# Up projections by feature with high and low tokens side by side, their halves summed in the eviction

## What is computed

```python
def sq_relu_mlp(h, w1, w2):                  # both layers of the first block; D_FF = 4096
    return jnp.square(jax.nn.relu(h @ w1)) @ w2

# second block, token mixer: three convolution inputs of 512 features each
proj = h @ w_in[l]
b_gate, c_gate, hc, q, k, v = jnp.split(proj, splits, axis=-1)
u = c_gate * hc                              # then a causal convolution of 3 taps
y = b_gate * conv(u)

# second block, PEER: product keys
q = (ht @ wq).reshape(t, PEER_HEADS, 2, PEER_DK)      # 2048 features
sa = jnp.einsum('thd,hnd->thn', q[:, :, 0], keys[0])
sb = jnp.einsum('thd,hnd->thn', q[:, :, 1], keys[1])
# top 16 of each, top 16 of their sums; then gelu(u_tab[i] . h) weights rows of v_tab
```

## Time and profile before

| | |
|---|---|
| time, median of 3 | 1451.2 us |
| the profiled execution | 1444.85 us |
| its span | 1443.0 us |
| TensorE busy | 1395.3 us, 97% |
| VectorE busy | 1128.4 us, 78% |
| ScalarE busy | 773.0 us, 54% |
| GpSimd busy | 388.2 us, 27% |
| mean DMA rate | 252 GB/s |

### The profile page before, as it was taken

One profiled execution on the slowest core, in us unless ns is written; L12 is line 12 of the kernel. 1 busy time (PEld: TensorE's weight loads), 2 busy tenths in 40 slices (PEclk: granted clock), 3 DMA queues, 4 the chain that ended last, 5 costly groups with the idle time before them and its releaser, 6 DMA issues.

```text
span 1443.0 us, 28261 instructions
## 1 busy us (share of the span) xinstructions
PE 1395.3 (97%) x10898; PEld 1295.1 (90%) x10898; DVE 1128.4 (78%) x2308; ACT 773.0 (54%) x1580; POOL 388.2 (27%) x421
## 2 busy tenths in 40 slices
PE   7899999998999999999989999999999999999998
PEld 6677998877879988888889999999999999999998
DVE  5676996787668889866657998676677698989897
ACT  6785886853255555567454212343343366656565
POOL 5720001000200000001100024687877334234330
PEclk9999999999999999999999999999999999999999
DMA  7205555651369899843434699999999999999995
GB/s 254 90 31 167 176 167 149 196 179 60 123 206 352 297 339 347 281 151 98 134 124 142 192 371 338 386 379 355 368 353 356 327 345 351 340 320 357 345 334 193
DMA packets 100147, 363.41 MB, mean 252 GB/s; under 512 B 11168, under 2 KB 11296, under 8 KB 99888
## 3 DMA queue, kind: packets, MB, share of 16 engines
q1 hardware_dynamic: 67680, 244.40, 49.1%
q0 software_dynamic: 24560, 89.95, 17.2%
q10 hardware_dynamic: 7776, 27.27, 5.3%
HBM read 360.52 MB, written 1.05 MB: 251 GB/s over the span
## 4 chain that ended last, share of the span: by engine, by line
PE 71%; DMA 10%; DVE 10%; ACT 4%; issue 3%; POOL 2%; ACTq 0%; DVEq 0%; SPq 0%
PE ps L630 69%; DMA arena<-in_peer_v 6%; DVE w_lo L1353 4%; DVE arena L1353 2%; DVE arena L1359 2%; ACT w_hi L2268 2%; DMA arena<-in_peer_u 2%; ACT arena L2265 1%; DMA arena<-in_u_rows,arena 1%; POOL arena L3007 1%; PE ps L836 1%; POOL arena L2999 1%; DVE act_hi_lo L1353 1%; PE ps L963 0%; DMA arena<-in_small 0%
## 5 line engine op out<-in xcount | busy, mean ns | idle before, releaser
L1353 DVE TENSOR_TENSOR w_lo<-arena,w_hi 128x512 fp32r<-128x512 f32 x680 | 456.5, 690 | 162.6 <-ACT w_hi L2268 157.1
L2268 ACT ACTIVATE w_hi<-arena 128x512 fp32r<-128x512 f32 x680 | 417.6, 625 | 287.8 <-PE ps L630 222.7
L630 PE MATMUL ps<-act_hi_lo,w_hi 128*128 128x256 f32 (+1 forms) x2496 | 554.7, 315 | 11.2 <-DVE w_lo L1353 4.0
L630 PE MATMUL ps<-arena 128*128 128x176 f32 (+10 forms) x4890 | 476.7, 278 | 15.0 <-issue 6.2
L630 PEld LDWEIGHTS ps<-arena 128*128 128x128 f32 (+2 forms) x4890 | 449.6, 163 | 37.9 <-issue 17.5
L630 PE MATMUL ps<-act_hi_lo,w_lo 128*128 128x176 f32 (+1 forms) x1760 | 455.8, 259 | 0.1
L630 PEld LDWEIGHTS ps<-act_hi_lo,w_hi 128*128 128x128 f32 x2496 | 421.2, 190 | 20.8 <-ACT w_hi L2268 7.5
L630 PEld LDWEIGHTS ps<-act_hi_lo,w_lo 128*128 128x128 f32 x1760 | 336.3, 191 | 0.1
L630 PE MATMUL ps<-w_hi,act_hi_lo 128*128 128x512 f32 (+2 forms) x960 | 302.7, 390 | 11.4 <-DVE w_lo L1353 3.9
L1353 DVE TENSOR_TENSOR arena<-arena 128x512 f32<-128x512 f32 (+14 forms) x312 | 183.8, 598 | 63.1 <-ACT arena L2265 55.2
L630 PEld LDWEIGHTS ps<-w_hi,act_hi_lo 128*128 128x128 f32 x960 | 180.1, 189 | 54.3 <-issue 12.9
(11 more groups left out here) (102 smaller groups left out, 664.6 us busy)
## 6 DMA issues: line engine op xcount, KB each, us to landing
arena<-in_w_ff SPq DMA_DIRECT2D x128, 512.0 KB
arena<-in_peer_u SPq DMA_DIRECT2D x128, 512.0 KB
arena<-in_peer_v SPq DMA_DIRECT2D x128, 512.0 KB
arena<-in_w_ada ACTq DMA_DIRECT2D x48, 512.0 KB, 6.1
arena<-in_w_glu SPq DMA_DIRECT2D x16, 512.0 KB
arena<-in_peer_wq SPq DMA_DIRECT2D x16, 512.0 KB
arena<-in_w_in SPq DMA_DIRECT2D x12, 512.0 KB
arena<-in_w_conv SPq DMA_DIRECT2D x12, 512.0 KB
```

The source lines that it names most:

```text
L630: return e.matmul(o, l, r, start=start, stop=stop)
L1353: return e.tensor_tensor(o, a, b, op)
L2268: return e.activation(o, a, ACT.Copy)
```

## The change

In `lin_T` and `first_pair` the three products of a k become two. The high weights meet the high and the low tokens side by side, 2 x 256 = 512 columns, which fills a bank: its first half gets high x high, its second half high x low. The low weights meet the high tokens, 256 columns, and add to the first half. A bank thus holds one unit (m) instead of a pair, and m chooses the bank. The halves are summed in the eviction, per unit: ScalarE copies the second half to SBUF (`low_out`), VectorE adds the first half from PSUM onto it and frees the bank (`halves`). Relu and square of the feed-forward are both ScalarE's now, in SBUF, each 512 wide, one pair behind: the relu after unit m = 0 of the next pair, the square after m = 1. VectorE no longer squares. All four stages are changed, the first layer's with them.

```diff
+    HX = act_hl[:, :].rearrange("p (h k t) -> p k h t", h=2, k=8)
 ...
+        def both(o, h, l, k, first, last):
+            whole, high = o, o[:, 0, :]
+            if last:
+                mm(high, l, HH[:, k, :], False, False)
+                return mm(whole, h, HX[:, k], False, True)
+            mm(whole, h, HX[:, k], first, False)
+            return mm(high, l, HH[:, k, :], False, False)
 ... first_pair
-                    ins = three(pb(0, 2, 256)[:, half, :], (h[:, kk, :], l[:, kk, :]), (HH[:, k, :], HL[:, k, :]),
-                                k == 0 and half == 0, k == 7 and half == 1)
+                    ins = both(pb(half, 2, 256), h[:, kk, :], l[:, kk, :], k, k == 0, k == 7)
 ...
-            bank[0].take(e, *use)
+            bank[0].take(e, *use, 0)
             piece(a, 0, 0).then_inc(*w_used())
             b, c = chunk(name), chunk(name)
+            bank[1].take(e, *use, 1)
 ... lin_T
-                if c == 0 and half == 0:
+                if c == 0:
                     bank[bk].take(e, *use)
 ...
-                    ins = three(pb(bk, 2, tokens)[:, half, :], (h[:, kk, :], l[:, kk, :]),
-                                (HH[:, k, 0:tokens], HL[:, k, 0:tokens]), k == 0, k == 7)
+                    ins = both(pb(bk, 2, 256), h[:, kk, :], l[:, kk, :], k, k == 0, k == 7)
 ... VectorE
+        def halves(o, bk, *event):
+            e.wait_ge(*low_half[event])
+            tt(o, pb(bk, 2, 256)[:, 0, :], o, ALU.add).then_inc(bank[bk].sem, 1)
 ... VectorE, ffn: after each unit, behind ada_step
-                d = aT[:, 2 * j:2 * j + 2, :]
-                e.wait_ge(*bank[j % 2]["ff1", layer, j])
-                tt(d, d, d, ALU.mult).then_inc(*relu2(layer, j))
+                    halves(aT[:, 2 * j + m, :], m, "ff1", layer, j, m)
 ... VectorE, conv: after each unit
+                    halves(cvT[:, 2 * j + m, :], 6 + m, "conv", j, m)
 ... VectorE, PEER queries
+        g, first = 0, end["peer_wq"] - 32
         for n in range(15):
             run(lin_T())
+            while at["n"] >= first + 2 * g + 2:
+                halves(qp[:, g, :], g % 2, "peer_q", g // 2, g % 2)
+                g += 1
             if n >= 6:
                 next(side)
 ... ScalarE
+        def low_out(o, bk, used, *event):
+            e.wait_ge(w_used.sem, used)
+            copy(o, pb(bk, 2, 256)[:, 1, :]).then_inc(*low_half(*event))
 ... ScalarE, ffn
+            def bend(j):
+                d = V(512 * j, 2, 256)
+                for m in range(2):
+                    e.wait_ge(*bank[m]["ff1", layer, j, m])
+                act(d, d, ACT.Relu).then_inc(*bent_half(layer, j))
+
+            def squares(j):
+                d = V(512 * j, 2, 256)
+                e.wait_ge(*bent_half[layer, j])
+                act(d, d, ACT.Square).then_inc(*relu2(layer, j))
             for j in range(16):
 ...
                     if layer == 1:
                         ada_step(m)
+                    low_out(V(512 * j + 256 * m, 256), m, first + (3 + m if j == 0 else 4 * j + 2 * m + 2),
+                            "ff1", layer, j, m)
+                    if j > 0:
+                        (bend, squares)[m](j - 1)
                 if j == 15:
                     e.wait_ge(w_used.sem, end[f"ff1_{layer}"] - 1)
                     cut_pair(f"ff2_{layer}", 0, V(0, 2, 256), ready)
-                e.wait_ge(w_used.sem, end[f"ff1_{layer}"] - 64 + 4 * (j + 1))
 ...
-                act(V(512 * j, 2, 256), pb(j % 2, 2, 256), ACT.Relu).then_inc(bank[j % 2].sem, 1)
+            bend(15)
+            squares(15)
 ... ScalarE, conv (the queries likewise)
-                e.wait_ge(w_used.sem, end["w_conv"] - 24 + 4 * (j + 1))
-                copy(cvT[:, 2 * j:2 * j + 2, :], pb(bk, 2, 256)).then_inc(bank[bk].sem, 1)
+                    low_out(cvT[:, 2 * j + m, :], 6 + m, end["w_conv"] - 24 + 4 * j + 2 * m + 2, "conv", j, m)
 ... GpSimd: each product of the convolution waits for the unit that it needs last
-        for c, j in enumerate((1, 2, 4, 5)):
+        for c, (j, m) in enumerate(((1, 0), (2, 1), (4, 0), (5, 1))):
-            e.wait_ge(*bank[6 + j % 2]["conv", j])
+            e.wait_ge(*bank[6 + m]["conv", j, m])
```

More of the change, by code:

```diff
@@ L196, in build_in @@
     relu2 = signal("relu_squared")
+    low_half = signal("low_halves")
+    bent_half = signal("relus")
     tab_v = signal("tables_vector")
@@ L739, in lin_tok_by_tiles, with lin_T @@
                         yield
-        def lin_T(name, bk, half, ready, *use, tokens=256):
+        def lin_T(name, bk, ready, *use):
             for c in range(2):
                 h, l = [x.rearrange("p (k n) -> p k n", k=4) for x in chunk(name)]
-                if c == 0 and half == 0:
+                if c == 0:
                     bank[bk].take(e, *use)
@@ L948, in ffn @@
                     if j > 0:
-                        for _ in lin_T(f"ff1_{layer}", j % 2, m, ready, "ff1", layer, j):
+                        for _ in lin_T(f"ff1_{layer}", m, ready, "ff1", layer, j, m):
                             next(side, None)
@@ L1081, in conv @@
                 for m in range(2):
-                    yield from lin_T("w_conv", 6 + j % 2, m, ready, "conv", j)
+                    yield from lin_T("w_conv", 6 + m, ready, "conv", j, m)
                 yield
@@ L1130, in scores @@
                 e.wait_ge(keys_in, 32)
-            e.wait_ge(*bank[1]["peer_q", 2 * b + 1])
+            e.wait_ge(*bank[1]["peer_q", 2 * b + 1, 1])
             for t in (1, 0):
@@ L1314, in tensor_program @@
             for m in range(2):
-                run(lin_T("peer_wq", j % 2, m, h_ready, "peer_q", j))
+                run(lin_T("peer_wq", m, h_ready, "peer_q", j, m))
             if j in (2, 4, 6):
@@ L2211, in vector_program @@
         side = pick(1)
+        g, first = 0, end["peer_wq"] - 32
         for n in range(15):
             run(lin_T())
+            while at["n"] >= first + 2 * g + 2:
+                halves(qp[:, g, :], g % 2, "peer_q", g // 2, g % 2)
+                g += 1
             if n >= 6:
                 next(side)
+        while g < 16:
+            halves(qp[:, g, :], g % 2, "peer_q", g // 2, g % 2)
+            g += 1
         run(side)
@@ L2565, in ffn @@
                     ada_fetch(n)
+            first = end[f"ff1_{layer}"] - 64
+            def bend(j):
[7 more added lines that the diff above has]
+                act(d, d, ACT.Square).then_inc(*relu2(layer, j))
             for j in range(16):
+                if j == 12:
+                    e.wait_ge(*squared["norm", s])
                 for m in range(2):
@@ L2581, in ffn @@
                     square(s, 1, V(7168, 1024)).then_inc(*squared("norm", s))
-                elif j == 12:
-                    e.wait_ge(*squared["norm", s])
-                act(V(512 * j, 2, 256), pb(j % 2, 2, 256), ACT.Relu).then_inc(bank[j % 2].sem, 1)
+            bend(15)
+            squares(15)
             down(f"ff2_{layer}", 32, lambda j: V(512 * j, 2, 256), ready, ada_step if layer == 1 else None, side)
@@ L2739, in conv @@
             for j in range(6):
-                bk = 6 + j % 2
                 for m in range(2):
                     yield from lin_T()
-                e.wait_ge(w_used.sem, end["w_conv"] - 24 + 4 * (j + 1))
-                copy(cvT[:, 2 * j:2 * j + 2, :], pb(bk, 2, 256)).then_inc(bank[bk].sem, 1)
+                    low_out(cvT[:, 2 * j + m, :], 6 + m, end["w_conv"] - 24 + 4 * j + 2 * m + 2, "conv", j, m)
                 yield
@@ L2936, in scalar_program @@
         norm(5, stat("gain2", 8), modT[:, 2, :])
+        first = end["peer_wq"] - 32
         for j in range(8):
@@ L2940, in scalar_program @@
                     run(lin_T())
-            e.wait_ge(w_used.sem, end["peer_wq"] - 32 + 4 * (j + 1))
-            copy(qp[:, 2 * j:2 * j + 2, :], pb(j % 2, 2, 256)).then_inc(bank[j % 2].sem, 1)
+                if j > 0:
+                    low_out(qp[:, 2 * j + m, :], m, first + 4 * j + 2 * m + 2, "peer_q", j, m)
+                elif m == 1:
+                    low_out(qp[:, 0, :], 0, first + 3, "peer_q", 0, 0)
+                    low_out(qp[:, 1, :], 1, first + 4, "peer_q", 0, 1)
             if j in (2, 4, 6):
```

## The result

The changed kernel took 1462.4 us (median of 4 runs, 1456.9 to 1463.5) against 1451.1: ratio 1.0084 [1.0061, 1.0108], slower. Run again later with more rounds it took 1457.7 against 1449.6, ratio 1.0060 [1.0036, 1.0084], which is 8.7 us [5.2, 12.2]. The forecast was +0.4 us, and its range of 1445 to 1458 holds the second of these medians by 0.3 us and misses the first by 4.4.

The account below looks back on a forecast made before the run. TensorE was taken to bound the kernel, busy 97% of the span. First layer +4.3, second -1.8, convolution -0.9 and PEER -1.2 gave +0.4 us: median 1451.6, range 1445 to 1458.

Parts of the forecast that it names:

- A pair of 347 ns: TensorE, all four stages: 227 + 120 ns per pair against 360 per triple, 0.053 us less a chunk, -9.8 us together.
- the far bound: TensorE's pairs: on the last stage's terms of alternating products, 371 ns a pair, +8 us over all.
- rival (c): TensorE's pairs outside the first layer: alternation costs 371 ns as in the last stage, +11.5 us, 1463; chance 0.04.
- rival (d): TensorE's pairs outside the first layer: a pair saves only 2.5 ns, +5.2 us, 1456.8; chance 0.03.
- First layer: +4.3: First up projection: +3.0 us to 224.2 from ScalarE's added work, -0.4 after it, +1.65 at the end.
- the end: End of each up projection: TensorE waits for the down projection's first cut, +1.65 us first layer, +1.35 second.
- The hand layout of the round: First up projection: twelve chunks laid out in order, ScalarE waiting 0.45 and 0.95 us, 19.3 us against 19.0.
- Rival (a): First up projection: the evictions hide there too, -5.6 us in all, 1445.6; chance 0.20.
- rival (b): First up projection: ScalarE and VectorE bind in turn, rounds 20.0 to 20.4 us, stretch +7.5, 1456.1; chance 0.23.
- Second layer: -1.8: Second up projection: -3.4 us from the pairs, +0.3 stalls, +1.35 at its end.
- Convolution: -0.9: Convolution's input: -1.3 us from the pairs, +0.4 given back as its last two banks wait for VectorE.
- PEER: -1.2: PEER queries: -1.7 us from the pairs, +0.5 for sums ahead of the top-16 steps and the start.

Follow-up runs that it names:

- p2: New form in the second layer's up projection alone, its low-weight products also 512 columns from the second pair of units on: 1.813 us a chunk.
- f2: Kernel before with the new form in the first layer's up projection alone, squares left out: rounds 18.67 and 18.65 us, stretch 104.33 us.
- e2: The changed kernel with the old form kept in the PEER queries: 1457.3 us, ratio to before 1.0059.
- q1: The changed kernel with VectorE's top-16 steps ahead of the sums in the PEER queries: 1457.1 us, ratio to before 1.0045.
- q0: The kernel before with the new form in the PEER queries alone: 1450.3 us, ratio 1.0005.
- t1: The changed kernel with the down projection's first cut ahead of the last unit's copy and preceding square, both layers: 1452.1 us, ratio to before 1.0026.
- b1: Kernel before with the new form in second layer's up projection and convolution's input, second layer's first down-projection cut moved earlier: 1446.0 us, ratio 0.9972.
- b2: b1 plus the new form in the PEER queries, with top-16 steps ahead of the sums: 1446.2 us, ratio to before 0.9974.

## Why the prediction was wrong

The direction of each cost was seen; the gains that were to pay for them were half of what was forecast. The sum was +0.4, the stretches give +6.5. By its own terms:

- **A pair of 347 ns: the step that failed.** It was put together from a wide product among wide ones and a narrow one among narrow ones; both figures hold (p2: 226.7, before: 120.0), but mixed they take 352.5 at best and 354 on average over the stage. So a chunk gains 0.025 us and not 0.053. Where the sum counted on it (second layer, convolution, PEER and the last seven chunks of the first) that is -3.2 us in place of -6.8: 3.6 of the 6.1 us, the largest part., a mixed stream already in the trace, said that a mixed pair costs more, and stood only as the far bound and as rival (c) at 371. The truth lay between the forecast's 347 and rival (d)'s 357. The Trainium skill ("TensorE: Matmul & The Clock Gate", section "Wait — 56ns, not 53.3ns?") has some 2.5 ns as a product's fixed cost, by which the pair would be an estimated 357; as a cost of each product the streams of one width contradict it with their 13 ns.
- **First layer: +4.3, measured +5.4.** Up to the first block of transposes +1.95 (forecast +2.0); the rounds 20.12, 19.29 and 19.31 where 19.3 was forecast, so +1.7 in place of +1.0, and the surplus all in the first round, which still works off the start; behind them -0.2 in place of -0.4; the end +1.87 in place of +1.65. The hand layout of the round held, and not by luck: its two waits of ScalarE for VectorE are in the trace (0.84 and 0.42 us), and a round of 19.3 held by ScalarE doesn't depend on what a pair costs TensorE, whose own round is 18.7 (f2). That sum and round agree to 0.01 us is luck, since the waits came out 0.14 shorter and the work 0.2 longer. Rival (a) fell, and rival (b) too: but for the first, rounds were not 20 us.
- **Second layer: -1.8, measured 0.0.** Chunks -1.6 in place of -3.4, the end +1.55 in place of +1.35, stalls nothing in place of +0.3.
- **Convolution: -0.9, measured -0.4.** The pair again (-0.6 in place of -1.3).
- **PEER: -1.2, measured +1.5.** The other large part. The pair gives -0.8 in place of -1.7. Of the sums in front of the top-16 steps I priced one (0.3 + 0.2); each of the last two held VectorE back, 1.35 and 1.19 us, and the picks came 1.3 us late. And the first sums wait: TensorE was held 1.07 us for a cut (745.12) that wasn't late before. That ScalarE's first two copies, which stand ahead of that cut and wait for the whole second unit, are its reason is read from the order, not tested.
- **The clock was left out.** A down projection that starts after a wait of 1.86 or 2.43 us sometimes starts at a lower granted clock. In the repeat of the changed kernel, the ten us around the first start, and then the same ten of the first profile:

```profile
244.25:254.25 10.00, 8.14 (x57) 5.79 (x56) 4.42 (x11) 6.54 (x13) 0.00 (x0) 0.83 0.27 95
```
```profile
244.35:254.35 10.00, 8.14 (x63) 6.10 (x62) 5.48 (x13) 7.66 (x15) 0.00 (x0) 1.00 0.33 106
```

The same busy time and the same wait, but 0.83 against 1.00, which is the 1.2 GHz level for a third of these ten us; that down projection takes 92.35 us in place of 90.80. Over the 17 profiles of this study it happened in 5 of the 14 starts with a wait of 1.86 or 2.43 us, and in none of the 20 with less (none to 1.34 us). At 1.55 us each, that adds on average 1.1 us to a kernel with both waits: an estimated 7.6 of the 8.7 measured.

The unprofiled executions bear it out too, since the mean granted clock of every one is on record. It is 0.9951 over 34 executions of the kernels with both waits (the changed one twice, e2, q1) and 0.9966 over 136 of those with neither (before, q0, t1, b1, b2). t1 differs from the changed kernel only in the order at these two places and has 0.9970 over 12, the changed kernel 0.9951 over 12. Within one kernel, 0.001 less clock goes with 1.1 us more (a fit over 206 executions), so 0.0015 are an estimated 1.7 us. It also explains in part why t1 gained 4.9 us where its stretches give 3.2, and why the first measurement was so high: its one execution at 0.999 took 1456.9 us, the three at 0.994 took 1461.9 to 1463.5. What is left of the 8.7 lies within the interval, and I can't name it.

The range was too narrow for the same reason: the far bounds of the pair (+8 us) stood in the text, but its rivals (c) and (d) had 0.07 of the chance together, as if the earlier trace rows were an exception. That the measured times come near those of rivals (b), 1456.1, (d), 1456.8, and (c), 1463, is chance: neither rounds of 20 us nor pairs of 357 or 371 ns were found.

## What to carry to other kernels

The spacing of an instruction among its like is no price for it in a mixture. Where the trace has one mixed stream, give the figure from there a real share of the chance: here it said 371 ns, the uniform streams 347, and 352.5 to 354 was measured. An eviction that goes from one helper instruction to three and stands in front of a cut must be paid for by an engine with room to spare, so a rewrite like this is made stage by stage (here it pays in the second layer, once the cut at its end is moved forward, and in the convolution). A step that waits for the last product belongs behind everything in its queue that is ready, and a wait of TensorE of about 2 us costs more than its length when the clock falls with it.

## What the runs showed of the hardware

- A product of 512 columns whose moving operand is two separate runs of 256 takes 226.7 ns, as with one run.
- Products of one width start at equal distances (120 ns, all of 283 in 34 us near the end of the kernel before's second up projection; 226 or 227 ns, all of 149 in p2's). With 512 and 256 mixed the distances spread over 224 to 242 and 112 to 121 ns, in a pattern that repeats with every unit, and a pair takes 352.5 ns, grouped by two 350.9.
- TensorE's granted clock fell at 5 of 14 starts that followed an idle of 1.86 or 2.43 us (2 of 5 and 3 of 9), at a cost of 1.55 us each, in the same code whose other executions kept 1.00, and at none of 20 that followed an idle of 1.34 us or less.
